# First delta-branch convolution tile run in three parts inside the samples' local attention

## What is computed

```python
xn = rmsnorm(x, p["norm_mix_g"])
aq, ak, av, dq, dk, dvv, dz, da, db, ga, gb = split_cols(xn @ p["w_in"], IN_SPLITS)
...                                   # rotary on aq, ak
    ya = swa_prompt(aq, ak, av, p["sinks"])                      # prompt
...
    ya, new_wk, new_wv = swa_sample(aq, ak, av, p["sinks"], win[0], win[1], pos)   # samples
qkv, new_dn_buf = causal_dwconv(jnp.concatenate([dq, dk, dvv], axis=-1), dn_buf, p["dn_conv_w"])
...                                   # silu, l2norm, decay g and beta from da, db
o, new_S = gated_delta(qh, kh, heads(dvv), g, beta, dn_state, chunk)
...                                   # gated mix of the two branches, memory attention, conv MLP
```

## Time and profile before

| | before |
|---|---|
| median of 3 runs | 2003.51 us (2002.65 to 2005.77) |
| span of the profiled execution | 2002.1 us |
| PE busy | 94% of the span |
| DVE, ACT, POOL busy | 48%, 24%, 42% |
| mean granted clock of TensorE | 0.991 |

### The profile page before, as it was taken

One profiled execution on the slowest core, in us unless ns is written; L12 is line 12 of the kernel. 1 busy time (PEld: TensorE's weight loads), 2 busy tenths in 40 slices (PEclk: granted clock), 3 DMA queues, 4 the chain that ended last, 5 costly groups with the idle time before them and its releaser, 6 DMA issues.

```text
span 2002.1 us, 32389 instructions
## 1 busy us (share of the span) xinstructions
PE 1891.3 (94%) x13273; PEld 1781.6 (89%) x13273; DVE 958.1 (48%) x1150; ACT 489.9 (24%) x908; POOL 832.1 (42%) x907
## 2 busy tenths in 40 slices
PE   6988999999999899999998899999999999999997
PEld 5966799988878788998988599999999999999996
DVE  6877267754454132554142437443453444345346
ACT  6056326643232103421132423100100010000012
POOL 3411033421211233745753025654654565465455
PEclk9999999999999999999999999999999999999999
DMA  4311111110102131422223101111111111111112
GB/s 186 91 38 44 35 43 42 32 65 23 37 27 69 31 107 34 148 96 96 74 76 146 63 26 43 43 42 52 42 42 47 47 42 42 52 42 42 52 46 87
DMA packets 45483, 119.72 MB, mean 60 GB/s; under 512 B 3808, under 2 KB 20896, under 8 KB 44224
## 3 DMA queue, kind: packets, MB, share of 16 engines
q1 hardware_dynamic: 45392, 118.39, 17.7%
HBM read 102.94 MB, written 15.77 MB: 59 GB/s over the span
## 4 chain that ended last, share of the span: by engine, by line
PE 68%; DVE 7%; ACT 3%; issue 1%; POOL 0%; DVEq 0%; ACTq 0%; POOLq 0%
PE PS L544 42%; PE PS L1987 12%; PE PS L1378 3%; PE PS L1576 2%; PE PS L1870 1%; PE PS L1614 1%; PE PS L1770 1%; DVE XL L524 1%; ACT TMP L1223 1%; PE PS L1934 1%; DVE H L2650 1%; PE PS L1955 1%; PE PS L2019 1%; PE PS L1661 0%; PE PS L1927 0%
## 5 line engine op out<-in xcount | busy, mean ns | idle before, releaser
L767 POOL TENSOR_TENSOR WH<-RAW,CST 128x256 fp32r<-128x256 f32 x288 | 195.1, 705 | 827.4 <-PE PS L544 407.0
L544 PE MATMUL PS<-XH,WH 128*128 128x352 f32 x2280 | 505.3, 330 | 33.7 <-POOL WL L759 13.2
L544 PE MATMUL PS<-XH,WL 128*128 128x352 f32 x2280 | 493.0, 324 | 0.0
L544 PE MATMUL PS<-XL,WH 128*128 128x352 f32 x2280 | 492.4, 324 | 0.0
L544 PEld LDWEIGHTS PS<-XH,WH 128*128 128x128 f32 x2280 | 389.2, 190 | 51.7 <-issue 34.5
L544 PEld LDWEIGHTS PS<-XH,WL 128*128 128x128 f32 x2280 | 392.6, 188 | 0.0
L544 PEld LDWEIGHTS PS<-XL,WH 128*128 128x128 f32 x2280 | 388.7, 188 | 0.0
L771 POOL TENSOR_TENSOR WL<-RAW,WH 128x256 fp32r<-128x256 f32 x288 | 260.3, 931 | 7.5
L2615 DVE TENSOR_TENSOR H<-H,PS 128x1056 f32<-128x1056 f32 x80 | 100.3, 1254 | 130.5 <-PE PS L1987 130.5
L757 POOL TENSOR_TENSOR WH<-RAW,CST 128x1024 fp32r<-128x1024 f32 x22 | 45.2, 2055 | 265.2 <-PE PS L544 140.9
L1285 ACT ACTIVATE AH<-TMP 128x1056 fp32r<-128x1056 f32 x20 | 20.8, 1082 | 359.0 <-PE PS L1987 345.6
(11 more groups left out here) (464 smaller groups left out, 2683.8 us busy)
## 6 DMA issues: line engine op xcount, KB each, us to landing
RAW<-in_w SPq DMA_DIRECT2D x136, 512.0 KB, 3.5
H<-in_xT SPq DMA_DIRECT2D x4, 1056.0 KB, 9.1
TMP<-in_xT SPq DMA_DIRECT2D x2, 2112.0 KB, 8.5
early_gates<-DV SPq DMA_DIRECT2D x18, 176.0 KB, 1.9
out_yT<-H SPq DMA_DIRECT2D x4, 704.0 KB
early_gates<-A SPq DMA_DIRECT2D x12, 176.0 KB, 1.8
DV<-early_gates SPq DMA_DIRECT2D x1, 2112.0 KB, 14.2
TMP<-early_gates SPq DMA_DIRECT2D x2, 1056.0 KB, 5.4
```

The costliest lines, as they stand in the source:

```text
L544: mm = nc.tensor.matmul(PS[:, 3 * mm_g + c, 0:CW], w_[:, p, off + k * P:off + (k + 1) * P], x_[:, xk0 + k, c * CW:(c + 1) * CW], start=fir ...
L767: nc.gpsimd.tensor_tensor(WH[:, p, c], RAW[:, p, c], one[:, 0:PIECE], ALU.mult)
```

## The change

The first tile of the `dn` stage (tile 0, accumulator in banks 0 to 2) no longer runs in one piece behind the samples' attention. Its eight steps are cut in three parts: steps 0 to 2 ahead of the transposes of the probabilities, steps 3 to 5 between these and the value products, steps 6 and 7 behind the value products. The transposes move from banks 0 to 4 to banks 3 to 7, since tile 0 now accumulates in banks 0 to 2; the attention output moves to a free part of bank 7; so PE waits for the third chunk of the decay inputs (`ab_row`) before the transposes, and ACT copies that chunk out (`gate_rows(2)`) before the copies of the probabilities. The value products run with `k` outside and the key group inside, so that neighbouring instructions write different halves of the output partitions.

```diff
@@ ACT
             gate_rows(1)
+            gate_rows(2)
             for b in range(4):
                 act.wait_ge(ss_tp, b + 1)
...
-            gate_rows(2)
             act.wait_ge(ss_pv, 1)
@@ PE
             gate_products(2)
+
+            def dn_first(a, b):
+
+                for k in range(a, b):
+                    mm = gemm_part(0, 0, k, KT)
+                    if k == KT - 1:
+                        mm.then_inc(w_used, 1)
+            pe.wait_ge(w_split, SLOTS["dn"][0] + 1)
+            pe.wait_ge(acc_free, acc0["dn"])
+            pe.wait_ge(ss_msk, 2)
+            dn_first(0, 3)
             pe.wait_ge(ss_p, 1)
+            pe.wait_ge(ab_row, 3)
...
-                    mm = nc.tensor.transpose(PS[0:rows, i // 4, (i % 4) * CH:(i % 4) * CH + CH],
+                    mm = nc.tensor.transpose(PS[0:rows, 3 + i // 4, (i % 4) * CH:(i % 4) * CH + CH],
...
+            dn_first(3, 6)
             pe.wait_ge(ss_pt, 5)
-            for g in range(2):
-                for k in range(NB):
-                    nc.tensor.matmul(PS[HD * g:HD * g + HD, 5, 0:CH], s_vc[:, k, HD * g:HD * g + HD], s_pt[:, k, g, :],
-                                     start=(k == 0), stop=False)
...
+            for k in range(NB + 1):
+                for g in range(2):
+                    v = s_vc[:, k, HD * g:HD * g + HD] if k < NB else s_v[0:TS, HD * g:HD * g + HD]
+                    pt = s_pt[:, k, g, :] if k < NB else s_pt[0:TS, NB, g, :]
+                    mm = nc.tensor.matmul(PS[HD * g:HD * g + HD, 7, 256:256 + CH], v, pt, start=(k == 0), stop=(k == NB))
             mm.then_inc(ss_pv, 1)
+            dn_first(6, KT)
...
-            pe.wait_ge(ss_y, 1)
-            pe.wait_ge(ss_pt, 5)
...
-            dn_tile(0, 0, False)
             dn_tile(1, 1, False)
```

More of the change, by code:

```diff
@@ L906, in _ @@
                 nc.scalar.activation(s_pt[:, 2 * b:2 * b + 2, :, :],
-                                     PS[:, b, :].rearrange("p (k g n) -> p k g n", k=2, g=2),
+                                     PS[:, 3 + b, :].rearrange("p (k g n) -> p k g n", k=2, g=2),
                                      ACT.Copy).then_inc(ss_pt, 1)
             act.wait_ge(ss_tp, 5)
-            nc.scalar.activation(s_pt[0:TS, 8, :, :], PS[0:TS, 4, 0:256].rearrange("p (g n) -> p g n", g=2),
+            nc.scalar.activation(s_pt[0:TS, 8, :, :], PS[0:TS, 7, 0:256].rearrange("p (g n) -> p g n", g=2),
                                  ACT.Copy).then_inc(ss_pt, 1)
-            gate_rows(2)
             act.wait_ge(ss_pv, 1)
-            nc.scalar.activation(YA[:, :, TP:T], PS[:, 5, 0:CH].rearrange("p (j n) -> p j n", j=NJ),
+            nc.scalar.activation(YA[:, :, TP:T], PS[:, 7, 256:256 + CH].rearrange("p (j n) -> p j n", j=NJ),
                                  ACT.Copy).then_inc(ss_y, 1)
@@ L1457, in _ @@
                     mm.then_inc(ss_tp, 1)
+            dn_first(3, 6)
             pe.wait_ge(ss_pt, 5)
-            for g in range(2):
-                for k in range(NB):
-                    nc.tensor.matmul(PS[HD * g:HD * g + HD, 5, 0:CH], s_vc[:, k, HD * g:HD * g + HD], s_pt[:, k, g, :],
-                                     start=(k == 0), stop=False)
-                mm = nc.tensor.matmul(PS[HD * g:HD * g + HD, 5, 0:CH], s_v[0:TS, HD * g:HD * g + HD],
-                                      s_pt[0:TS, NB, g, :], start=False, stop=True)
+            for k in range(NB + 1):
[3 more added lines that the diff above has]
+                    mm = nc.tensor.matmul(PS[HD * g:HD * g + HD, 7, 256:256 + CH], v, pt, start=(k == 0), stop=(k == NB))
             mm.then_inc(ss_pv, 1)
-            pe.wait_ge(ab_row, 3)
+            dn_first(6, KT)
             for c in range(NBLK):
```

## The result

The changed kernel is faster by about 0.3%. Over 19 runs of each, the median is 1998.84 us (1995.15 to 2003.98) against 2005.07 us (2001.77 to 2009.77), and the ratio is 0.9972 with a 95% interval of 0.9964 to 0.9980, that is 5.6 us (4.0 to 7.2); the two medians lie 6.2 us apart. Forecast were 6.2 us less and 1997.3 us.

The account below looks back on a forecast made before the run. PE was taken as the bound; 2.34 + 1.95 + 2.1 - 0.2 = 6.2 us less takes 2003.5 to 1997.3 us, with a range of 1995.5 to 2000.5 us.

Parts of the forecast that it names:

- What bounds the kernel: PE busy for 94% of the span; the `dn` stage goes at PE's pace, so gains ahead of it are kept.
- (a): PE's idle wait for DVE's division, ahead of the transposes: covered by steps 0 to 2, gain 2.34 us.
- (b): Transposes and ACT's copies behind them: 1.98 us at full clock instead of 3.93, gain 1.95 us.
- (c): Value products: alternating halves overlap, 2.5 us instead of 4.60, gain 2.1 us.
- (d): Two more changes between tile 0's rounded operands and full fp32 ones, 0.1 us each: -0.2 us.
- limit in between: Value products: issue of weight loads, 0.07 us each, so 36 records need some 2.4 us at least.
- upper bound of the gain: Value products: 18 steps of 0.11 us plus 0.4 us, 2.4 us in all, a gain of 2.2 us.
- Rival B: Halves take turns in the value products, gaining only 0.3 us there: 4.4 us less, 1999.1 us; chance 0.12.
- Rival E: A change of half drains the array at 17 changes between value products: 0.7 us slower, 2004.2 us; chance 0.04.
- Rival C: Clock falls elsewhere: one low stretch, 1.1 to 1.7 us, in or behind the passage: 1998.6 us; chance 0.10.
- Rival D: The `dn` stage or the one behind it has its own pace: time as before, 2003.5 us; chance 0.06.
- What is late next: Behind tile 0: decay chain 4.2 us, ACT's copy done at 249.6, 7 us to spare before tile 2.

Follow-up runs that it names:

- the fill alone: Changed kernel, but value products again by key group (nine of group 0, then nine of group 1): passage 19.16 us, ratio to before 0.9980 (0.9967 to 0.9993).

## Why the prediction was right, and where its sizes were off

**What bounds the kernel.** Right. Behind the passage ACT, DVE and POOL still wait for PE. What ended the idle time from 250 to 425 us in the changed kernel, to set beside the earlier trace rows (POOL's first wait falls ahead of the window now; ACT's copies of tiles 0 and 2 and DVE's convolutions of tiles 0 and 1 start late and without a wait, all others wait as before):

```profile
POOL WH L757 <- PE PS L544: 75.4, 9, 9.1
ACT TMP L935 <- PE PS L544: 57.0, 10, 9.8
DVE TMP L2218 <- ACT TMP L942: 35.7, 10, 4.9
```

**The sum.** Against the second profile of the kernel before, which has no low stretch, term by term: (a) the idle time, 2.35 us, forecast 2.34. (b) transposes and the wait behind them, 3.03 - 1.88 = 1.15 us, forecast 1.95. (c) value products, 4.50 - 2.27 = 2.23 us, forecast 2.1. (d) more seams: tile 0 in three parts takes 4.37 + 4.54 + 3.10 = 12.01 us, and in one piece, from 239.68 us to the start of tile 1, it took 11.71:

```profile
251.39 0.65 PE L544 MATMUL PS<-XH,WH 128*128 128x352 f32 x3
```

That is -0.30 us, forecast -0.2. Together 5.4 us, and 22.37 - 16.93 = 5.44. Against the first profile, from which the forecast was made, the terms are 2.34, 2.05, 2.33 and -0.26 us, 6.46 in all. The run times (4.0 to 7.2 us less) have room for both numbers and for a mean of them, so they confirm the forecast of 6.2 us only within that width.

**The step that was mis-sized** is (b): "The granted clock of the piece is 0.60, that is, most of it at the lower level of 1.2 GHz, right behind PE's 2.3 idle microseconds". I counted its cost as a property of the kernel. It is one of an execution: 1.02 us in this kernel, in one of its two profiles, and in three of six over all kernels with the idle time, so about 0.5 us on average, on few cases. One profile can't tell the two apart. That the forecast of 6.2 us met the 6.2 us between the medians so closely is in part luck: the first profile happened to hold the low stretch, and the sum was 0.26 us below what that profile then gave.

**Smaller slips.** In (c) the "limit in between", 2.4 us by issue, and the upper bound of the gain, 2.2 us, were both passed: 36 records took 2.27 us. The low end of the range takes 0.3 us off for that upper bound, where (c) allows 2.2 - 2.1 = 0.1. And the chances of being faster (0.68 and 0.10 nearly always, two thirds of 0.12) add up to as much as 0.86, where 0.80 is written, with no reason for the 0.06 between.

**Rival B** (halves take turns) fell with the 2.27 us of the changed kernel, beside the 4.50 us of the fill alone, which is what B describes. The rule that was set against (c) (the Trainium skill, "TensorE: Matmul & The Clock Gate", section "Packing small matmuls — row/col tiling") would have given those 4.50 us; the measured 2.27 us go against it here. **Rival E** (a drain at each change of half) fell the same way. **Rival C** is right in kind: the first profiled executions of the changed kernel and of the one before differ by low stretches elsewhere. By the mean clocks of 0.989 and 0.991, some 22 and 18 us were lost to them over the span, 1.7 of the 18 in the passage itself. That leaves an estimated 5.7 us more outside the passage, where 5.5 are to be explained; the last digit of the clock is worth 1 us either way in each. The windows show some of those of the changed kernel, and then the same stretches before:

```profile
1032.00:1040.00 8.00, 7.31 (x32) 6.88 (x33) 5.49 (x5) 0.00 (x0) 0.00 (x0) 0.79 0.50 193
656.00:664.00 8.00, 7.61 (x52) 7.26 (x53) 4.19 (x13) 0.79 (x3) 0.00 (x0) 0.79 0.13 35
108.00:112.00 4.00, 4.00 (x20) 3.30 (x17) 3.06 (x10) 2.71 (x12) 0.00 (x0) 0.57 0.27 103
764.00:768.00 4.00, 4.00 (x11) 2.18 (x10) 0.94 (x1) 0.94 (x1) 0.00 (x0) 0.63 0.37 131
```

```profile
1032.00:1040.00 8.00, 5.77 (x33) 5.19 (x34) 8.00 (x6) 1.81 (x3) 0.97 (x1) 1.00 0.58 197
656.00:664.00 8.00, 5.62 (x57) 5.04 (x56) 2.40 (x6) 2.15 (x6) 2.53 (x4) 1.00 0.33 99
108.00:112.00 4.00, 3.95 (x29) 3.25 (x26) 3.06 (x10) 3.59 (x14) 0.00 (x0) 1.00 0.32 123
```

The one at 108 us lies ahead of anything that the change touches, and is why the passage began at 229.12 and not at 228.16. So in that pair of profiles 1.0 us was gone before the passage and 4.5 us behind it. In a second pair, taken later, it is 2007.4 against 1999.3 us. Which executions get which stretches stays open. The change isn't the cause of those ahead of it, and run times 4.0 to 7.2 us shorter leave no room for 4.5 us lost behind the passage every time. **Rival D** fell with the medians.

**What is late next** was right in its outcome and off in a size. I took the decay chain over as 4.2 us long. It took 7.3 us (246.16 to 253.45), 3.1 us of them more in two operations of DVE (last section), and ACT's copy of tile 0, behind it, ended at 253.5 instead of 249.6, no earlier than before (253.1). PE came to the decay matmuls at 257.8 and to tile 2 at 259.0, so 4.4 and 5.5 us of my 7 us of slack were left, and it never waited.

## What to carry to other kernels

Products that fill only a half or a quarter of the output partitions should be ordered so that neighbours in the program write different ones: here that cut the time to a half for halves and to 0.29 and 0.42 of it for quarters, and a record passed only some four of another half. Work moved over a wait was worth the wait here (2.35 us for the first, 0.94 for the second), and a low stretch of clock behind it only as often as it comes, so take several profiles before a one-time stretch goes into a sum. The first reordering, worth two microseconds, pointed to the larger ones: look for every other place with the same loop order.

## What the runs showed of the hardware that was not expected

Four column quarters with their own weight loads run fully side by side: 128 pairs of load and matmul in 3.75 us, 0.029 us a pair.

Two small operations of DVE, 36 columns wide, took 1.07 and 2.44 us in the changed kernel, where such operations take 0.20 and 0.18 us. The timeline of DVE and of POOL:

```profile
246.46 1.07 DVE L2181 TENSOR_TENSOR TMP<-TMP,CST 128x36 f32<-128x36 f32 x1 [14.22 <-ACT TMP L921]
247.57 2.44 DVE L2182 TENSOR_SCALAR TMP<-TMP 128x36 f32<-128x36 f32 x1
245.59 1.89 POOL L757 TENSOR_TENSOR WH<-RAW,CST 128x1024 fp32r<-128x1024 f32 x1 [25.87 <-PE PS L544]
247.56 2.41 POOL L759 TENSOR_TENSOR WL<-RAW,WH 128x1024 fp32r<-128x1024 f32 x1
```

Each of the two ends within 0.1 us of the end of a POOL operation that ran beside it (247.48 and 249.97). The second profile of the changed kernel has them at 1.08 and 2.44 us. The change brought them there: tile 0's last matmul now comes just ahead of the decay chain, and POOL starts to split the next slot at that moment. The same thing stood at another place before: there POOL's split comes later, the decay operations take 0.20 and 0.18 us, and it is a 32-column operation of the convolution that takes 2.38 us and ends within 0.1 us of POOL's (256.54 and 256.49). In the changed kernel the same operation (L2219) has no POOL beside it and takes 0.24 us. The kernel before first, then the changed one:

```profile
254.16 2.38 DVE L2210 TENSOR_SCALAR TMP<-TMP,CST 128x32 f32<-128x32 f32 x1
253.77 2.72 POOL L759 TENSOR_TENSOR WL<-RAW,WH 128x1024 fp32r<-128x1024 f32 x1
```

```profile
255.03 0.24 DVE L2219 TENSOR_SCALAR TMP<-TMP,CST 128x32 f32<-128x32 f32 x1
```

So the long times go with POOL's work and not with the operation. No run took POOL's work away; that DVE is held until POOL is done is the reading that fits all of these, and not shown beyond them.
